# Moving the sample state's update and the settled columns' norms from the end of a mixer into the levels of its triangular inverse

## The reference, cut to what matters

```python
parts = [rms_norm(o_a, out_g[0]),                                  # windowed attention
         rms_norm(o_b, out_g[1]),                                  # forgetting attention
         rms_norm(o_c, out_g[2]) * silu(heads(z_c)),               # gated delta rule
         rms_norm(o_d, out_g[3])]                                  # gated MLP
return concatenate(parts, axis=2).reshape(n, l, 1024) @ w_out
```

## Time and profile before

| | us |
|---|---|
| three executions | 1549.21, 1551.33, 1551.56 (median 1551.33) |
| the profiled execution, its own time | 1548.85 |
| the span in its trace | 1547.0 |
| TensorE busy | 1315.4 (85%) |
| VectorE busy | 926.5 (60%) |
| ScalarE busy | 600.7 (39%) |
| GpSimd busy | 233.4 (15%) |

### The profile page before, as it was taken

One profiled execution on the slowest core, in us unless ns is written; L12 is line 12 of the kernel. 1 busy time (PEld: TensorE's weight loads), 2 busy tenths in 40 slices (PEclk: granted clock), 3 DMA queues, 4 the chain that ended last, 5 costly groups with the idle time before them and its releaser, 6 DMA issues.

```text
span 1547.0 us, 27736 instructions
## 1 busy us (share of the span) xinstructions
PE 1315.4 (85%) x9864; PEld 1218.1 (79%) x9864; DVE 926.5 (60%) x1524; ACT 600.7 (39%) x1023; POOL 233.4 (15%) x232
## 2 busy tenths in 40 slices
PE   6999979984696479999989999799756757799998
PEld 5999979963375379999989999799534636799996
DVE  4766455478654756664476654555866555666643
ACT  4664453243000255443556544434410003544444
POOL 1000011017341330000110000200444331200000
PEclk9999989976587589999989999899657967899998
DMA  6565563545462244555646645454355513355563
GB/s 222 178 194 156 168 201 113 156 127 167 130 182 65 75 131 141 187 180 150 192 139 188 190 147 171 146 168 138 97 179 170 157 43 110 109 180 178 159 172 99
DMA packets 286118, 234.14 MB, mean 151 GB/s; under 512 B 19898, under 2 KB 282018, under 8 KB 286056
## 3 DMA queue, kind: packets, MB, share of 16 engines
q1 hardware_dynamic: 286056, 233.37, 49.7%
HBM read 228.65 MB, written 5.37 MB: 151 GB/s over the span
## 4 chain that ended last, share of the span: by engine, by line
PE 68%; DVE 16%; issue 6%; SPq 3%; POOL 3%; ACT 2%; DMA 2%; DVEq 0%; POOLq 0%; ACTq 0%
PE ps L1445 19%; PE ps L1446 19%; PE ps L1447 19%; DVE wlo L919 2%; POOL kslot L888 2%; PE ps L1673 2%; DVE nlo L966 2%; DVE s L1166 1%; PE ps L1762 1%; DVE yt L949 1%; ACT whi L600 1%; SPq L431 1%; PE ps L1761 1%; DMA raw<-in_w_in_dram 1%; PE ps L1809 1%
## 5 line engine op out<-in xcount | busy, mean ns | idle before, releaser
L1445 PE MATMUL ps<-nhi,whi 128*128 128x264 f32 x1936 | 562.8, 291 | 44.6 <-DVE nlo L966 34.1
L919 DVE TENSOR_TENSOR wlo<-raw,whi 128x1024 fp32r<-128x1024 f32 (+2 forms) x376 | 395.2, 1092 | 274.4 <-ACT whi L600 274.0
L1446 PE MATMUL ps<-nlo,whi 128*128 128x264 f32 x1936 | 557.1, 288 | 0.0
L1447 PE MATMUL ps<-nhi,wlo 128*128 128x264 f32 x1936 | 556.3, 287 | 0.0
L1445 PEld LDWEIGHTS ps<-nhi,whi 128*128 128x128 f32 x1936 | 373.6, 193 | 51.6 <-DVE nlo L966 27.2
L600 ACT ACTIVATE whi<-raw 128x1024 fp32r<-128x1024 f32 (+2 forms) x376 | 336.9, 945 | 188.6 <-PE ps L1447 112.3
L1446 PEld LDWEIGHTS ps<-nlo,whi 128*128 128x128 f32 x1936 | 373.8, 193 | 0.2
L1447 PEld LDWEIGHTS ps<-nhi,wlo 128*128 128x128 f32 x1936 | 371.7, 192 | 0.0
L1445 PE MATMUL ps<-hhi,whi 128*128 128x264 f32 x704 | 201.9, 287 | 9.1 <-DVE hlo L936 9.1
L1447 PE MATMUL ps<-hhi,wlo 128*128 128x264 f32 x704 | 200.8, 285 | 0.0
L1446 PE MATMUL ps<-hlo,whi 128*128 128x264 f32 x704 | 200.3, 285 | 0.0
(11 more groups left out here) (334 smaller groups left out, 1415.3 us busy)
## 6 DMA issues: line engine op xcount, KB each, us to landing
raw<-in_ffn_gate_dram SPq DMA_DIRECT2D x44, 1024.0 KB, 5.3
raw<-in_ffn_up_dram SPq DMA_DIRECT2D x44, 1024.0 KB, 5.3
raw<-in_ffn_down_dram SPq DMA_DIRECT2D x64, 704.0 KB, 4.6
raw<-in_w_in_dram SPq DMA_DIRECT2D x24, 1024.0 KB, 5.8
kslot<-in_cache_fox_k_dram SPq DMA_DIRECT2D x128, 128.0 KB, 2.7
vslot<-in_cache_fox_v_dram SPq DMA_DIRECT2D x128, 128.0 KB, 2.5
raw<-in_w_out_dram SPq DMA_DIRECT2D x8, 1024.0 KB, 5.2
kslot<-in_state_swa_k_dram SPq DMA_DIRECT2D x32, 128.0 KB, 2.7
```

The costliest lines, as they stand in the source:

```text
L919: tt2(wlo[s][:, a:b], raw[s][:, a:b], whi[s][:, a:b].bitcast(F32), ALU.subtract).then_inc(S(f"w_lo{s}"), 1)
L1445: mm(out, wh, hi_, start=first, stop=False)
L1446: mm(out, wh, lo_, start=False, stop=False)
L1447: return mm(out, wl, hi_, start=False, stop=last)
```

## The change

The samples' state is stepped between the levels, and at the end only what depends on the delta rule or on the last pair of samples is left.

- SyncE loads `state` before the keys of samples 4 and 5, no longer after `qkt`. The stores of the prompt's new state move from before the first `w_out` load to behind the state's trip through DRAM.
- GpSimd makes the products of state with key (`skp_of(0)`, before sample 4's keys), of key with new value (before sample 6's keys) and of state with query (`skp_of(1)`, after sample 7's). It norms all columns but the delta rule's in `norm_early`, before sample 6's keys.
- ScalarE makes the sums of squares for these columns itself, by 28 activations with an accumulator, right after `tm_act`, and their inverse roots.
- VectorE has four more steps in `between`, sums `skp` once more after `vn`, and norms the delta rule's columns itself.
- TensorE has the two products that add partitions at level 2 (counting from 0) and after `ks_mm`, and does six of the eight products of `so_mm` at level 5.
- The decay is now part of two later instructions, so that its own instruction (line 1373) is gone; `sk_r` has its own place.

```diff
 # SyncE
+                    for b in range(B): sp.dma_start(state[...], io["state_gdn_s"][b, l]...)   # then keys 4, 5
-                    sp.wait_ge(S("qkt"), V("qkt", 2))
-                    for b in range(B): sp.dma_start(state[...], io["state_gdn_s"][b, l]...)
...
-                    sp.wait_ge(S("p_state"), V("p_state", 4))
-                    for h in range(H): sp.dma_start(o["gdn_s_prompt"][0, l, h], st_s[...]).then_inc(st, 16)
...
                     sp.dma_start(smp_o[:, 512:768], d_oc).then_inc(S("oc_in"), 16)
+                    sp.wait_ge(S("p_state"), V("p_state", 4))
+                    for h in range(H): sp.dma_start(o["gdn_s_prompt"][0, l, h], st_s[...]).then_inc(st, 16)
                     sp.wait_ge(S("s_state_out"), V("s_state_out", 16 * B))
                     sp.wait_ge(S("stored"), V("stored", 16 * 18))
                     wo(0, 1)
 # ScalarE, after tm_act
+                    act.wait_ge(S("state_in"), V("state_in", 16 * (B + 4 + 2 + 4)))
+                    act.activation(small[:, 120:121], gb[:, 0:1], ACT.Exp).then_inc(S("sg"), 1)
+                    act.wait_ge(S("o_mm"), ...); act.wait_ge(S("o_att"), ...); act.wait_ge(S("mix_d"), V("mix_d", 2))
+                    for t in range(NT):
+                        for k, h in enumerate((0, 1, 2, 3, 4, 5, 6, 7, 12, 13, 14, 15)):
+                            ins = act.activation(..., otok[:, t, h * HD:(h + 1) * HD], ACT.Square, accum_out=small[:, 64 + 16 * t + h:65 + 16 * t + h])
+                    ch(ins)
+                    for h in range(H):
+                        ins = act.activation(..., smp_o[:, 768 + h * HD:768 + (h + 1) * HD], ACT.Square, accum_out=small[0:B, 108 + h:109 + h])
+                    ch(ins)
+                    ...  # three Ln, three Exp -> mix_r 4
                     sample_exp(2)
                     sample_exp(3)
...
-                    act.wait_ge(S("s_out"), V("s_out", 1))
-                    act.wait_ge(S("s_state_out"), V("s_state_out", 16 * B))
+                    act.wait_ge(S("oc_mm"), V("oc_mm", 2))
                     hi("wo", 0, 0)
+                    ...  # Ln, Exp for mix_ss 5 and for mix_ss 6
                     hi("wo", 0, 1)
 # GpSimd
+                    def skp_of(k):
+                        ...  # waits state_in or s_state
+                        tt_(skp, state, kq16[:, 1 - k, :]..., ALU.mult).then_inc(S("sk_prod"), 1)
+                    def norm_early():
+                        pool.wait_ge(S("mix_r"), V("mix_r", 4))
+                        for a, b in ((0, 512), (768, 1024)):
+                            v = otok[:, :, a:b].rearrange("p t (h d) -> p t h d", d=HD)
+                            ch(tt_(v, v, r[:, :, a // HD:b // HD]..., ALU.mult))
+                            tt_(otok[:, :, a:b], otok[:, :, a:b], both(a, b), ALU.mult)
+                        ...  # smp_o[:, 768:1024] by norm and gain
+                        tt_(smp[:, ZC:ZC + GW], smp[:, ZC:ZC + GW], og[0:B, 512:768], ALU.mult)
+                        tt_(tok[:, :, ZC:ZC + GW], tok[:, :, ZC:ZC + GW], both(512, 768), ALU.mult).then_inc(S("mixed"), 1)
                     for b in range(B):
+                        if b == 4:
+                            skp_of(0)
+                        if b == 6:
+                            norm_early()
+                            pool.wait_ge(S("v_new"), V("v_new", 1))
+                            tt_(skp, kq16[:, 1, :]..., v64[:, :]..., ALU.mult).then_inc(S("sk_prod"), 1)
...
+                    skp_of(1)
-                    ...  # squares and scaling of otok, 1024 columns wide, two tiles (lines 893 to 903)
 # VectorE
+                    def state_sum(k):     # waits sk_prod 2k+1
+                        red(sk_r[:, :], skp[:, :, :].rearrange("p k v -> p v k"), AX.X, ALU.add).then_inc(S("sk"), 1)
+                    def state_value():    # waits sg, sk_mm 1
+                        ch(stt(v64[:, :], ps[:, 6, 0:HD], eb, v64[:, :], ALU.mult, ALU.subtract))
+                        ts(v64[:, :], v64[:, :], gb[:, 1:2], None, ALU.mult).then_inc(S("v_new"), 1)
+                    def state_new():      # waits sk_prod 2
+                        stt(state[:, :, :], state[:, :, :], eb, skp[:, :, :], ALU.mult, ALU.subtract).then_inc(S("s_state"), 1)
+                    def sample_three():   # waits so_mm 1
+                        dve.tensor_copy(smp_o[:, 0:512], ps[0:B, 6, :]).then_inc(S("so"), 1)
-                    between = {0: [sample_add(5), sample_bias(2)], 1: [sample_shift(2)], 2: [sample_out(2)],
-                               3: [sample_add(6)], 4: [sample_add(7), sample_bias(3)], 5: [sample_shift(3)]}
+                    between = {0: [sample_add(5), sample_bias(2)], 1: [sample_shift(2), state_sum(0)],
+                               2: [state_value, sample_out(2)], 3: [state_new, sample_add(6)],
+                               4: [sample_add(7), sample_bias(3)], 5: [sample_shift(3), sample_three]}
...
                     dve.tensor_copy(vn[:, 0, :], ps[:, 0, 0:GW]).then_inc(S("vn"), 1)
+                    state_sum(1)
...
+                    dve.wait_ge(S("sk_mm"), V("sk_mm", 2))
+                    dve.tensor_copy(v64[:, :], ps[:, 6, 0:HD]).then_inc(S("s_out"), 1)      # before vn of tile 1
+                    ...  # squares of otok[:, t, 512:768] (square_c), norm and gate of these columns -> mixed 2
+                    dve.wait_ge(S("oc_in"), V("oc_in", 16))
+                    smp_square(512, 768)
                     sample_out(3)
-                    ...  # lines 1367 to 1408: state, sums of squares, so, squares and norm of smp_o
+                    dve.wait_ge(S("mix_r"), V("mix_r", 6))
+                    smp_scale(512, 768)
+                    tt2(smp_o[:, 512:768], smp_o[:, 512:768], smp[:, ZC:ZC + GW], ALU.mult)
+                    dve.wait_ge(S("so_mm"), V("so_mm", 2))
+                    ch(tt2(smp_o[:, 0:512], smp_o[:, 0:512], ps[0:B, 5, :], ALU.add))
+                    smp_square(0, 512)
                     lo("wo", 0, 0)
+                    dve.wait_ge(S("mix_r"), V("mix_r", 7))
+                    smp_scale(0, 512)
+                    tt2(smp_o[:, 0:512], smp_o[:, 0:512], og[0:B, 0:512], ALU.mult).then_inc(S("mixed"), 1)
 # TensorE
+                        if k == 2:
+                            state_mm(0)                      # between the two groups of a level's products
+                        if k == 5:
+                            pe.wait_ge(S("v_new"), V("v_new", 1))
+                            to_tokens(6, (0, 1, 2))          # six of the eight products, before turn_max(3)
...
                     ins.then_inc(S("ks_mm"), 1)
+                    pe.wait_ge(S("so"), V("so", 1))
+                    state_mm(1)
                     pe.wait_ge(S("rhs1"), V("rhs1", 1))
...
                     sample_values(3)
-                    ...  # both state products and all eight of so_mm
+                    to_tokens(5, (3,))
                     pe.wait_ge(S("mixed"), V("mixed", 3))
```

More of the change, by code:

```diff
@@ L218, in build @@
         qkt = scratch("qkt", 1024, [P, 2, 512])
-        sk_r = place("sk_r", [P, HD], at=cursor[0])
         ys = scratch("ys", 1024, [P, 2, 512])
@@ L269, in build @@
         kq16 = place("kq16", [P, 2, 16])
+        sk_r = place("sk_r", [P, HD])
         v64 = place("v64", [P, HD])
@@ L277, in build @@
         v_own = scratch("v_own", 2 * (GW + 1), [B, 2, GW + 1])
-        squares = [a[:, :, :].rearrange("p t n -> p (t n)") for a in (tm, tt)]
         ps = ctx.enter_context(nc.psum_tensor("ps", [P, 8, 512], F32))
@@ L525, in _ @@
                         sp.dma_start(v64[c:P:4, :], d_cn[2].rearrange("b (h e) -> (b h) e", e=HD)).then_inc(S("state_in"), 16)
+                    for b in range(B):
+                        sp.dma_start(state[16 * b:16 * b + 16, :, :].rearrange("p k v -> p (k v)"),
+                                     io["state_gdn_s"][b, l].rearrange("h (c k) v -> (h c) (k v)", c=4)).then_inc(S("state_in"), 16)
                     for b in (4, 5):
@@ L529, in _ @@
                         keys(b)
-                    sp.wait_ge(S("qkt"), V("qkt", 2))
-                    for b in range(B):
-                        sp.dma_start(state[16 * b:16 * b + 16, :, :].rearrange("p k v -> p (k v)"),
-                                     io["state_gdn_s"][b, l].rearrange("h (c k) v -> (h c) (k v)", c=4)).then_inc(S("state_in"), 16)
                     for b in (4, 5):
@@ L544, in _ @@
                         vals(b)
-                    sp.wait_ge(S("p_state"), V("p_state", 4))
-                    for h in range(H):
-                        sp.dma_start(o["gdn_s_prompt"][0, l, h], st_s[64 * (h % 2):64 * (h % 2) + 64, h // 2, :]).then_inc(st, 16)
                     def wo(j, s):
@@ new lines, in _ @@
+                    ch(ins)
+                    for h in range(H):
```

(33 more changed lines are left out.)

122 lines of the change are left out of this document (57 added, 65 removed).

## The result

The changed kernel takes 1514.57 us (median of 4 executions, 1512.63 to 1516.91) against 1551.3 us of the kernel before. The ratio is 0.977, with a 95% interval of 0.976 to 0.978. The profiled execution took 1515.05 us with a span of 1513.2 us, which is 33.8 us less than before.

The account below looks back on a forecast made before the run. VectorE's serial list at the mixer's end, 29.4 us a layer, was taken as the bound. Giving back 22.0 less 4.65 us makes 17.35 us a layer, 34.7 us in all: 1516.6 us for the median, range 1509 to 1527 us.

Parts of the forecast that it names:

- The end: From the last pair's `oms` to TensorE's first transpose: 7.4 us in place of 29.4, giving back 22.0 us a layer.
- `state_sum(0)`: VectorE sum of 1.87 us before a mask that waits 0.42 us for TensorE: costs 1.45 us a layer.
- `state_new`: VectorE update before `sample_add(6)`, all on the path beside GpSimd's keys: costs 2.2 us, bounds 1.2 and 3.3.
- The bias collision: VectorE's `sample_bias(2)` as GpSimd begins `norm_early`: costs 1.0 us, bounds 0 and 5.7; a rival with more had chance 0.12.
- The rival of a falling clock: TensorE's clock falls for the whole of the levels; at c = 0.5 slower, 1584 us; chance 0.03.
- Last-level products: Six products at the last level, where TensorE waits 2.83 us for maxima: cost nothing, up to 1.5 us as bound.
- the clock stays up: Rival: TensorE's filled last-level idle keeps levels at 2.4 GHz, about 2 us a layer gained, 1511 us; chance 0.08.
- The levels together: Added cost in the levels from `state_sum(0)`, `state_new` and the bias: 1.45 + 2.2 + 1.0 = 4.65 us a layer.
- Covers: Spare time hiding moved work: GpSimd's key products for samples 6 and 7 were to be hidden with 3 us to spare.
- The second `w_out` tile: Before ScalarE's first copy of a transposed tile: split done with 1 us spare; rival that it or DRAM gates, chance 0.10.
- best case: All terms at their favourable bounds: 21.9 us gained a layer, 1507.6 us.
- worst case: All terms at their unfavourable bounds: 8.1 us gained a layer, 1535 us.

Follow-up runs that it names:

- run 3: Against the changed kernel, GpSimd makes the outer product of key and new value six times instead of once: 1528.99 us.
- run 5: Against the changed kernel, `state_new` moved from behind level 3 into VectorE's wait behind level 2: 1511.77 us.
- run 4: Against the changed kernel, GpSimd starts `norm_early` only when the maxima of pair 2 are out, behind the bias: 1509.33 us.
- run 6: Against the changed kernel, twelve useless products added on TensorE at level 4, behind the wait for `v_new`: 1509.1 us.

## Why the prediction was right, step by step

The forecast of 1516.6 us is 2.0 us above what came. The mechanism was right: the end was VectorE's list, it left the end as listed, and it was hidden in the levels for the most part. That the number fits so well is partly luck. TensorE's clock, which the sum had left out, cost about 2.6 us a layer at levels 1 and 4 and gave 2.4 to 2.6 us a layer at the last level and in the delta part. For the profiled execution 1514.2 us was said and 1515.05 us came. The 2.5 us that were added for the median did not hold: this time the profiled execution is 0.5 us above the median.

- **The end** was forecast at 7.4 us and is 6.94 us. The four records take 1.04 us, not 1.36: TensorE ran them at a clock of 1.00, and the row that I took mixes both. The rest of the list is as written. It gives back 22.4 and 22.5 us, where 22.0 was said.
- **`state_sum(0)`** was to cost 1.45 us. Level 2 grew by 1.3 us, with the sum at 1.90 us. Right.
- **`state_new`** was to cost 2.2 us and cost 1.28 us, at the lower bound. It began 0.1 us before the end of a product of GpSimd, and GpSimd's next product lost 1.0 us, which its cover hid. In runs 3 and 5 it began 0.08 us behind the start of a product and took 2.27 us, the forecast value. So the order of the two within 0.2 us decided the price, which the prediction could not know.
- **The bias collision** was to cost 1.0 us with bounds of 0 and 5.7. It cost 1.65 us: two instructions lost 0.8 us each, and run 4 takes it away. The two copies lost nothing. `norm_early` began at 436.2 us, not at 439, since ScalarE's squares start 0.24 us apart and not 0.32, so GpSimd was in its second product. The Trainium skill (page "SBUF — State Buffer", section "Who interferes with whom") says that a VectorE instruction with two SBUF inputs contends with a GpSimd one that reads SBUF, and that the lock on the shared port pair is exclusive. The trace agrees: the two bias instructions end within 0.1 us of GpSimd's products. The first lost the rest of a running product, 0.8 us of 2.34 us; the second began 0.04 us behind the start of one and waited for nearly all of its 1.04 us.
- **TensorE's clock was left out of the sum, and that step failed.** VectorE's delays were priced by their own length. A delay of 1.28 us at level 4 brought 2.5 us of clock in layer 1 and 0.9 in layer 2, and level 1 lost 1.7 us to it in layer 2 (0.1 in layer 1, where it had fallen before). Runs 5 and 6 show it for level 4 by two different edits with the same value. The rival of a falling clock had the right mechanism and the wrong extent: it took the whole stretch at 0.5, while the clock falls for a part of two levels and leaves the mean at 0.83. The Trainium skill (page "TensorE: Matmul & The Clock Gate", section "HAM oscillation — how this bites in real kernels") tells of kernels that fall to the low clock at each gap. The runs agree for the long waits: at levels 1 and 4, in all traced runs, each time TensorE's longest wait was 3.69 us or more the level's mean clock was under 1.00. With a longest wait of 2.49 to 2.83 us it went both ways (7 times the level kept 1.00, 11 times it did not). With one of 1.01 us or less it stayed at 1.00.
- **Last-level products** were to cost nothing. The level became 1.4 and 1.6 us shorter: TensorE has work before the `z` products, which then run at the full clock, 2.05 us for 16 records. The delta part became 1.0 us shorter, at a mean clock of 0.73 in place of 0.65. These 2.4 and 2.6 us belong to the rival "the clock stays up", which came true for the last level and the delta part while the opposite came true for levels 1 and 4. That the early products are the cause fits the rows, but no run leaves them out.
- The levels together cost 6.05 and 5.59 us where 4.65 was said. Level 0, which had no term, has 0.7 and 0.4 us of this; it varies from 7.3 to 8.3 us between the traces. With the end's 0.4 and the delta part's 1.0 us on the other side, a layer gains 17.3 and 17.9 us, where 17.35 was forecast.
- **Covers.** GpSimd had 4.2 us to spare, of which a collision can take 1 us (run 3); 3 was said. The second `w_out` tile was issued 4.5 us later than said, since the stores of the prompt's state before it began at 500.37 us and not at 495.3. It had 1.7 us to spare instead of 1. No one waited for the trip through DRAM.
- **The bounds** have two slips. The 1.6 us of extra gain in the best case stand in no term of the sum, and the worst case takes 20 us for the end's gain, where 29.4 - 9 is 20.4 us. Neither moves the range by much.

It stays open why the same gap before the maxima lets the clock fall in one layer and not in the other.

## What to carry to other kernels

An engine's serial list can move from a stretch where TensorE waits into the idle time of an earlier stretch. Here that gave 22.4 us a layer at the end, and 17.3 to 17.9 us were left when all stages were paid. Price the host stretch by TensorE's granted clock as well: a vector instruction of 1.3 us on the alternating path cost 3.7 us at level 4. Look for the longest wait of TensorE in such a stretch, and shorten it by moving vector work to a place where VectorE already waits, or fill it with products of no use (here a wait cut to 1.01 us left the clock up, one cut to 2.54 us did not). Take several executions, since the clock's fall differs between them. Order two engines that share SBUF by one semaphore when short instructions of the one are on the path and long ones of the other have room.

## What the runs showed of the hardware

- Twelve products of no use in TensorE's gap made the levels 2.3 and 2.7 us shorter, although TensorE was the busiest engine (87%).
- The clock's fall isn't set by the code alone: level 1 took 9.69 us in layer 1 and 12.29 us in layer 2 of one kernel (run 4), and before it was the other way round (11.31 and 9.68 us). TensorE's wait before it was 2.83 us in all four.
- A short VectorE instruction that meets a running GpSimd product ends with it: 1.01 and 1.03 us instead of 0.23 and 0.18 us, and the copies behind them kept their 0.16 us.
